# Feed-forward up-projection of a hybrid decoder step: two of three token chunks as seven block products in place of eight, weights through a ring of eight 512-column units

## What is computed

```python
def conv_glu(x, conv_buf, g_norm, w_up, conv_w, conv_b, w_down):
    h = rmsnorm(x, g_norm)
    gate, val = jnp.split(h @ w_up, 2, axis=-1)
    gp = jnp.concatenate([conv_buf.astype(gate.dtype), gate], axis=1)
    T = gate.shape[1]
    gc = conv_b + sum(conv_w[j] * gp[:, j:j + T] for j in range(CONV_W))
    y = jax.nn.gelu(gc) * val
    return x + y @ w_down, gp[:, -(CONV_W - 1):]
```

## Time and profile before

| what | before |
|---|---|
| median of 3 runs | 3221.44 us (3221.01 to 3224.05) |
| span of the profiled execution, all the time the page gives for it | 3219.3 us |
| PE busy | 3117.2 us (97%), 19459 matmuls |
| DVE / ACT / POOL busy | 1854.2 / 1027.8 / 901.3 us |
| mean granted TensorE clock | 0.990 |

### The profile page before, as it was taken

The page is one execution under the profiler, slowest core; times in us unless marked ns, Lnnn a source line. Parts: engine busy times, 40 slices in busy tenths (PEclk is TensorE's granted clock), DMA queues, the critical chain, the costliest instruction groups (busy, mean ns, idle before and its releaser), DMA issues.

```text
span 3219.3 us, 50875 instructions
## 1 busy us (share of the span) xinstructions
PE 3117.2 (97%) x19459; PEld 2847.0 (88%) x19459; DVE 1854.2 (58%) x4369; ACT 1027.8 (32%) x2117; POOL 901.3 (28%) x2061
## 2 busy tenths in 40 slices
PE   7999999899999999999999999998999999999999
PEld 7887777599999999999987777766999999999998
DVE  5676465655555555557467755647555555555663
ACT  4444344533111111115344433455321111111251
POOL 3111122505322324223322210333232333223231
PEclk8999999999999999999999999999999999999999
DMA  5211234512111111110221111336111121111111
GB/s 172 55 47 49 56 83 120 177 51 66 40 53 40 40 66 40 53 40 21 94 69 47 47 50 48 109 106 195 53 40 40 40 66 40 53 40 40 40 37 71
DMA packets 228570, 208.87 MB, mean 65 GB/s; under 512 B 36676, under 2 KB 207620, under 8 KB 226736
## 3 DMA queue, kind: packets, MB, share of 16 engines
q1 hardware_dynamic: 228328, 205.62, 21.1%
HBM read 173.96 MB, written 31.61 MB: 64 GB/s over the span
## 4 chain that ended last, share of the span: by engine, by line
PE 87%; DVE 8%; ACT 2%; issue 1%; POOL 1%; DMA 1%; SPq 0%; DVEq 0%; ACTq 0%
PE ps L923 25%; PE ps L925 24%; PE ps L924 24%; PE ps L1095 2%; PE ps L1066 2%; PE ps L1081 2%; POOL wlo L868 1%; PE ps L1038 1%; PE ps L1216 1%; PE ps L1290 1%; DVE lo L1943 1%; DVE att L2112 1%; DVE att L2101 1%; PE ps L1199 0%; PE ps L1031 0%
## 5 line engine op out<-in xcount | busy, mean ns | idle before, releaser
L868 POOL TENSOR_TENSOR wlo<-raw,whi 128x128 fp32r<-128x128 f32 (+3 forms) x1952 | 857.1, 478 | 1833.4 <-ACT whi L1483 1404.9
L923 PE MATMUL ps<-hi,wlo 128*128 128x344 f32 x2880 | 927.8, 322 | 10.0 <-POOL wlo L868 8.1
L925 PE MATMUL ps<-hi,whi 128*128 128x344 f32 x2880 | 922.3, 320 | 0.0
L924 PE MATMUL ps<-lo,whi 128*128 128x344 f32 x2880 | 921.6, 320 | 0.0
L923 PEld LDWEIGHTS ps<-hi,wlo 128*128 128x128 f32 x2880 | 544.4, 189 | 13.6 <-POOL wlo L868 8.6
L925 PEld LDWEIGHTS ps<-hi,whi 128*128 128x128 f32 x2880 | 543.5, 189 | 0.0
L924 PEld LDWEIGHTS ps<-lo,whi 128*128 128x128 f32 x2880 | 542.9, 188 | 0.6
L923 PE MATMUL ps<-whi,lo 128*128 128x512 f32 (+3 forms) x1056 | 413.4, 391 | 4.8 <-POOL wlo L868 4.3
L925 PE MATMUL ps<-whi,hi 128*128 128x512 f32 (+3 forms) x1056 | 390.3, 370 | 0.0
L924 PE MATMUL ps<-wlo,hi 128*128 128x512 f32 (+3 forms) x1056 | 388.7, 368 | 0.0
L2530 DVE TENSOR_TENSOR X<-X,ps 128x344 f32<-128x344 f32 x528 | 268.0, 511 | 184.7 <-PE ps L925 182.9
(11 more groups left out here) (325 smaller groups left out, 3873.6 us busy)
## 6 DMA issues: line engine op xcount, KB each, us to landing
raw<-in_w_up SPq DMA_DIRECT2D x44, 1024.0 KB, 5.1
raw<-in_w_in SPq DMA_DIRECT2D x112, 256.0 KB, 4.4
raw<-in_w_down SPq DMA_DIRECT2D x22, 1024.0 KB, 4.9
kvb<-in_cache_win_k SPq DMA_DIRECT2D x48, 256.0 KB, 3.3
cache<-in_cache_win_v SPq DMA_DIRECT2D x42, 256.0 KB, 3.7
X<-x_scratch SPq DMA_DIRECT2D x4, 2064.0 KB, 11.1
raw<-in_w_out SPq DMA_DIRECT2D x8, 1024.0 KB, 8.5
raw<-in_w_ple_gate SPq DMA_DIRECT2D x8, 1024.0 KB, 5.2
```

What stands on the lines that cost most here:

```text
L868: pool.tensor_tensor(out=wlo[:, s, r], in0=raw[:, s, r], in1=whi[:, s, r].bitcast(F32), op=ALU.subtract).then_inc(w_split, 1)
L923: nc.tensor.matmul(out, a_lo, b_hi, start=first, stop=False)
L924: nc.tensor.matmul(out, a_hi, b_lo, start=False, stop=False)
L925: return nc.tensor.matmul(out, a_hi, b_hi, start=False, stop=last)
```

## The change

The feed-forward operand is now normed before the product: `h` = X times gain times rstd. For chunks 0 and 1 the up-projection is a 2x2 block product. Of the weights (hidden tile o by half of the 8 input tiles) the blocks are A11, A12, A21, A22; of `h` (half of the input tiles by chunk) B11, B21 for chunk 0 and B12, B22 for chunk 1. Sums of them are made beforehand:

- on GpSimd, for each block of weights: S1 = A21 + A22, S2 = S1 - A11, S4 = A12 - S2, S3 = A11 - A21;
- on GpSimd, once for each layer: T1 = B12 - B11, T2 = B22 - T1, T4 = B21 - T2, T3 = B22 - B12.

Seven products of 12 matmuls are left (named by their weights: A11, A12, S2, S1, S3, A22, S4), and their results are added up by VectorE from PSUM (`plus`), with a ScalarE copy of the first (`copied_base`). Chunk 2 is computed as before (`plain`), with half-blocks of 12 matmuls between the products. A block (gate or val) is then 84 + 48 = 132 matmuls. Weight units of 512 columns go through a ring of eight places (`unit_places`), rounded by `high_unit` on ScalarE and split by `low_unit` on GpSimd as one instruction each; a place is free when `done_with` says so. Two slots of `raw` take turns for gate, val and down. The embedding operands `ph`, `pl` are saved to DRAM and read back, since their tiles hold B22 and T3 meanwhile. The order of chunks in `down` is 2, 0, 1 except in the last group. Core of the diff:

```diff
-GEMM_PLE = GEMM_FFN + 36 * FG
+GEMM_PLE = GEMM_FFN + 24 * FG
+def done_with(u):
+    i, j = divmod(u, GROUP_UNITS)
+    if j >= 2 * RING:
+        return "gemm_done", GEMM_FFN + 24 * i + 2 * KT + (HALF if j < 2 * RING + 2 else KT)
+    n, x = 2 * i + j // RING, j % RING
+    if n == 0:
+        return "up_done", event(0, ("V0half", "V0", "P6", "P5", "V1", "P7", "V1", "P3")[x])
+    return "up_done", event(n, ("V0", "V0", "P6", "P5", "V1half", "P7", "P4", "P3")[x])
@@ SyncE
+                for m in range(3 * FG):
...
+                        sp.wait_ge(w_split, unit_split(l, GROUP_UNITS * i + (RING, 2 * RING, GROUP_UNITS)[kind] - 1))
@@ GpSimd
+                def up_block(n):
...
+                    low_unit(unit_of(n, "A11"), a11)
+                    low_unit(unit_of(n, "A12"), a12)
...
+                    step(pool.tensor_tensor(out=tiles4(s1), in0=a21, in1=a22, op=ALU.add), s_sum)
+                    step(pool.tensor_tensor(out=tiles4(s2), in0=tiles4(s1), in1=a11, op=ALU.subtract), s_sum)
+                    step(pool.tensor_tensor(out=a12, in0=a12, in1=tiles4(s2), op=ALU.subtract), s_sum, wait=False)
+                    step(pool.tensor_tensor(out=a11, in0=a11, in1=a21, op=ALU.subtract), s_sum)
+                    low_unit(unit_of(n, "S2"), s2)
+                    low_unit(unit_of(n, "S1"), s1)
+                    low_unit(unit_of(n, "A21"), a21)
+                    low_unit(unit_of(n, "S3"), a11)
+                    low_unit(unit_of(n, "A22"), a22)
+                    low_unit(unit_of(n, "S4"), a12)
@@ TensorE, first block of a layer
+                    product(0, "A11", "B11", 0, True).then_inc(up_done, 1)
+                    pe.wait_ge(*at(rstd_done, 2))
+                    sums(at, 1, 2)
+                    product(0, "A12", "B21", 0, False).then_inc(up_done, 1)
+                    product(0, "S2", "T2", 1, True).then_inc(up_done, 1)
+                    product(0, "S1", "T1", 2, True).then_inc(up_done, 1)
+                    product(0, "S3", "T3", 1, False).then_inc(up_done, 1)
+                    product(0, "A22", "T4", 4).then_inc(up_done, 1)
+                    product(0, "S4", "B22", 2, False).then_inc(up_done, 1)
+                    plain(0, "A11", True, False).then_inc(up_done, 1)
@@ TensorE, every other block: events P1, (half), P2, V0, P6, P5, V1half, P7, V1, P4, P3
+                def up_block(n):
...
+                    product(n, "A11", "B11", 0, True).then_inc(up_done, 1)
+                    plain(n, "A11", True, False)
+                    pe.wait_ge(*at(up_copy, copy_value(n, "P1")))
+                    product(n, "A12", "B21", 0, False).then_inc(up_done, 1)
+                    plain(n, "A12", False, True).then_inc(up_done, 1)
+                    product(n, "S2", "T2", 1, True).then_inc(up_done, 1)
+                    product(n, "S1", "T1", 2, True).then_inc(up_done, 1)
@@ VectorE
-                    do(v.tensor_tensor(out=w[:, 2:CH + 2], in0=ps[:, s % 3, 0:CH], in1=rstd[:, col(c)], op=ALU.mult), gate_read)
...
-                    do(v.tensor_tensor(out=y, in0=y, in1=rstd[:, col(c)], op=ALU.mult))
...
+                    plus(first_sum, base_copy(g), 1, up_read)
...
+                        if i == FG - 1 and c == 1:
+                            for k in range(KT):
+                                low(at, l, 2, 0, k)
```

More of the change, by code:

```diff
@@ L323, in build @@
         lo, lof = shared("lo", [P, KT, TOK], "vectors")
[L324 removed]
+        whi, whf = shared("whi", [P, NSLOT, WBLK], "weights")
         wlo, raw = shared("wlo", [P, NSLOT, WBLK], "raw")
@@ L917, in _ @@
+                for n in range(B_PLE, NBLK):
                     split(B + n)
@@ new lines, in product @@
+                def product(n, part, name, bank, first=True):
+                    w_h, w_l = unit_places(unit_of(n, part))[0:2]
+                    for k in range(HALF):
+                        b_h, b_l = operand(name, k)[0:2]
+                        if n == 0:
+                            pe.wait_ge(*at(split_lo, 24 + OPERAND_LOWS.index((name, k)) + 1))
+                        m = slice(k * P, (k + 1) * P)
+                        out = ps[:, bank, 0:CH]
+                        if first:
+                            mm = three(out, w_h[:, m], w_l[:, m], b_h, b_l, k == 0, k + 1 == HALF)
+                        else:
+                            mm = further(out, w_h[:, m], w_l[:, m], b_h, b_l)
+                    return mm
@@ new lines, in plain @@
+                def plain(n, part, first, last):
+                    o, h = int(part[1]) - 1, int(part[2]) - 1
+                    w_h, w_l = unit_places(unit_of(n, part))[0:2]
+                    for j in range(HALF):
+                        k = HALF * h + j
+                        if n == 0:
+                            pe.wait_ge(*at(t_sum, 16 + k + 1))
+                        m = slice(j * P, (j + 1) * P)
+                        mm = three(ps[:, 3 + o, 0:CH], w_h[:, m], w_l[:, m], hi[:, k, col(2)], lo[:, k, col(2)],
+                                   first and j == 0, last and j + 1 == HALF)
+                    return mm
@@ L1803, in _ @@
                         n = KT * c + o
-                        if c and o == 0:
-                            act.wait_ge(*at(gemm_done, GEMM_OUT + KT * c))
-                            for k in range(KT):
-                                high(l, 1, c - 1, k)
                         if c == 0 and o + 3 < NT:
@@ L2465, in _ @@
                         add_square(at, 1, KT * c - 1)
-                        for k in range(KT):
-                            low(at, l, 1, c - 1, k)
                     for o in range(KT):
@@ new lines, in _, with arrived, base_in, plus @@
+                first_sum, second_sum = rstd[:, col(0)], rstd[:, col(1)]
+                def arrived(n, name):
+                    dve.wait_ge(*at(up_done, event(n, name)))
+                def base_in(n):
+                    dve.wait_ge(*at(up_copy, copy_value(n, "P1")))
+                def plus(out, a, bank, sem, wait=True):
+                    do(v.tensor_tensor(out=out, in0=a, in1=ps[:, bank, 0:CH], op=ALU.add), sem, wait=wait)
+                def gate_place(o, c):
+                    return gw[:, o, 2 + c * CH:2 + (c + 1) * CH]
```

777 lines of the change are left out of this document (570 added, 207 removed).

## The result

| | before | after |
|---|---|---|
| median | 3221.66 us (3221.01 to 3224.05) | **3354.2 us** (3349.87 to 3356.75, 4 runs) |
| ratio | | **1.0404**, 95% interval 1.0389 to 1.0419 |
| span of the profiled execution | 3219.3 us | 3348.0 us |
| mean granted clock | 0.990 | 0.964 |

What follows compares the result with a forecast made beforehand. TensorE was taken to bound the kernel, busy for 3117.2 of 3219.3 us. 3219.3 - 83.1 + 6 + 45 + 8 = 3195.2 us of span, with 2.1 us to the median: 3197 us, 8-in-10 range 3164 to 3226.

Steps and rivals of the forecast that it cites:

- Part 1: Up-projection: 528 matmuls fewer at 0.1574 us each, 83.1 us less.
- Part 2: Other three engines in a steady group: none full, order decides; 6 us more for 20 groups.
- (a): In val, the second product waits for ScalarE's copy of the first: ready at 3.2 us, asked at 3.8, nothing charged.
- (b): Next gate's first unit rounded before y's high parts: down's low part ready about 40.5, asked for 41.6, nothing charged.
- (c): Start of down: VectorE's first addition ends at 44.6, the fourth output wants that bank at 44.4; 0.3 us charged.
- The prediction's own sign: Groups more than 65.6 us apart, or a start losing over 40 us, would make the prediction wrong.
- a wait in every group: Rival: val's copy comes late in each of 22 groups; 3232 us if the chain slips by 2.2 us; chance 0.15.
- Part 3: Start of the feed-forward, twice: waits for operands and lower clock, 22.5 us a layer, 45 us more.
- Four chains: Feed-forward start: waits on chunk 2's sum of squares 3 us, unit S3 5.1, unit A22 4.2, unit S4 4.3.
- The first product: Feed-forward start: it waits for the last tile of B11, there at 746.7; 5.0 us idle.
- chunk 2's low parts: Feed-forward start: eight low parts on GpSimd, 0.8 us each, follow unit S4; 1.5 us of waiting.
- Part 4: End of the feed-forward, twice: eight lows before chunk 1's first output is read; 8 us more, between 2 and 12.

Runs made afterwards that it cites:

- kernel 2: The changed kernel with three low parts of y moved behind VectorE's first additions of down: 3245.06 us, ratio 1.0066.
- edits 6 and 7: Each alone on kernel 2: ScalarE rounds weight units earlier at the feed-forward's start, 3214.27 us; VectorE's operand lows in order of use, 3240.71 us.
- experiment 9, second: Kernel 2 with edits 6 and 7 and two gate blocks' rounding moved to columns 2 and 3 of the embedding loop: 3202.91 us, ratio 0.9945.
- experiment 8: Kernel 2 with two gate blocks' rounding moved from ahead of a row root to columns 4 and 5 of the embedding loop: 3256.02 us, ratio 1.0106.

## Why the prediction was wrong

- **Part 1 (products removed) held.** 528 matmuls fewer at 0.1575 us; kernel 2's groups are 64.3 us apart, 64.2 predicted.
- **Part 2 (a) and (b) held.** The groups of kernel 2 between the first and the last have no idle time at all, so neither the copy in val nor the gate's first unit is late. GpSimd's piece of 512 columns takes 1.34 us, 1.2 taken.
- **Part 2 (c) is the step that failed.** It had VectorE's first addition of down end 3.0 us after val's end (44.6 - 41.6) and charged 0.3 us. In the last group, where GpSimd is idle, it ended 2.8 us after and TensorE waited 0.34. In the group shown it ended 5.5 us after (1041.18 - 1035.64), and in all ten groups before the last the wait came. A low part had been taken at 0.60; the last four took 4.7 us (2.81 + 0.96 + 0.94) where that gives 2.4, and the last multiplication of gelu's result by val 1.06 where the one before took 0.52. Together that is 2.8 us, a little more than the 2.5 by which the addition was late. The rows that bore on it, 0.50 against 0.69 in the earlier trace rows, were read as a share that a pass loses beside GpSimd, and I did not ask what it is beside instructions nearly three times as long. Both causes are needed: long passes, and their place in the queue. Taking away the second gives back 109 us; 20 groups x 5.0 us make 100 of it, 3.0 in the wait and 2.0 in the slow matmuls behind it. The prediction's own sign came up: groups 69.3 us apart, where more than 65.6 was to make it wrong.
- **The rival "a wait in every group" was the case**, by 0.15 of chance, and with its wait at another place (down's start, not val). It held 0.6 us of idle time "too short to matter" and named slow matmuls behind 1.6: a wait of 1.0 us left the clock alone, one of 1.85 and nearly all from 2.5 on did not. But its sum, 22 x 1.6 = 35 us, has no term for those matmuls, which at 2.6 us of waiting were another 1.6.
- **Part 3 (the start) named the right chains and was mis-sized: 39.4 and 39.9 us against 18.7.** Four chains came almost as worked out: 2.1 for 3, 5.1 for 5.1, 4.0 for 4.2, 4.0 for 4.3. The first product did not: 11.9 us idle in layer 0 for 5.0. It is the error of (c) again, a two-operand pass taken at 0.65 us where a low takes 1.2 to 1.5 beside GpSimd's sums, so that the last tile of B11 is there at 753.5 and not at 746.7. The 1.5 us for chunk 2's low parts did not show, the start of val took 4.2 for 2.5, and 1.1, 1.5 and 3.4 (the last is (c)'s wait) had no term here. The clock is the other part: 13.6 - 3.0 = 10.6 us where I added 3 and took off 2.1. 32.5 us more idle time (37.2 - 4.7) and 10.6 of clock, less the 3.8 saved, make 39.3 of the 39.4. Nearly half of it is order: kernel 2 with edits 6 and 7 (experiment 9, second) begins its first down 18.8 us sooner.
- **Part 4 (the end) was near for what it counted.** The eight lows take 4.6 us and TensorE waits 3.68 us behind them, 3 predicted. The whole last group of layer 0 idles 3.7 us more than before and its slow matmuls add 3.0 more, so it pays 7 where 4 was charged. The embedding, for which nothing was charged, costs 3.1 and 10.5 more, of which 7.9 are the one long pass shown above; kernel 2 has 3.2 and 3.4 there. The rounding of two gate blocks stands ahead of the row root that TensorE waits for (that wait fell by 4.7 us in experiment 8, but the time did not). How much of the 3 us it makes is open.
- **The forecast of 3197 us** is what the best kernel of experiment 9 comes to within 6 us. That is luck in part: it is another kernel, its start stretch is 15.7 and 14.0 us longer than before's (18.7 forecast), its last groups 5.3 and 4.7 (0.2 forecast), and its groups pay 0 in place of 0.3.

By the Trainium skill (GPSIMD Engine Reference, "Specifications") GpSimd and VectorE share memory interfaces for two-input work. The trace agrees and adds the size: VectorE's pass stretches from 0.46 us to about the length of GpSimd's instruction, 1.49 beside 1.42 to 1.53. Shorter GpSimd instructions alone gave 20 us; the order gave 109.

## What to carry to other kernels

When a change makes one engine's instructions longer, price its neighbours on a shared resource anew at that length, and lay the queue at each handoff out again with these durations. Ahead of the first instruction that frees a PSUM bank, an engine should carry nothing that isn't needed for it; moving three passes was worth 109 us, and cutting GpSimd's instructions instead 20. Count a stall by its length: here one of 1.0 us cost 1.2 times itself, and those of 2.6 and 3.0 us (means of nine groups) 1.6 to 1.7 times.
